# Turning q and k with transposing DMAs on 16-bit halves instead of TensorE transposes

## The reference

```python
for l in range(DEPTH):
    h = rms_norm(x, norm_mix[l])
    z = h @ w_in[l]
    qa, ka, va, qb, kb, vb, uc, gz = jnp.split(z, SPLIT_POINTS, axis=-1)
    qa = apply_axial_rope(rms_norm(qa.reshape(b, s, A_Q_HEADS, HEAD_DIM), qn_a[l]), ang_row, ang_col)
    ka = apply_axial_rope(rms_norm(ka.reshape(b, s, A_KV_HEADS, HEAD_DIM), kn_a[l]), ang_row, ang_col)
    ya = dense_gqa_blocked(qa, ka, va) @ w_branch_a[l]
    qb = apply_rope(rms_norm(qb.reshape(b, s, B_HEADS, HEAD_DIM), qn_b[l]), ang_seq)
    kb = apply_rope(rms_norm(kb.reshape(b, s, B_HEADS, HEAD_DIM), kn_b[l]), ang_seq)
    # B: three groups of four heads, each a dilated window; combined by their softmax denominators
    ...
    gates = jax.nn.sigmoid(gz + b_gate[l]).reshape(b, s, N_BRANCHES, D_MODEL)
    merged = gates[:, :, 0] * ya + gates[:, :, 1] * yb + gates[:, :, 2] * yc
    x = x + merged @ w_out[l]
    h2 = rms_norm(x, norm_ffn[l])
    x = x + (jax.nn.silu(h2 @ w_ffn_gate[l]) * (h2 @ w_ffn_up[l])) @ w_ffn_down[l]
```

## Time and profile before

| | us |
|---|---|
| runs: median (lowest to highest) | 822.84 (822.7 to 823.5) |
| profiled execution, device time | 823.74 |
| its span, first to last instruction | 821.9 |
| TensorE busy | 816.8 |
| VectorE busy | 574.0 |
| ScalarE busy | 436.4 |
| GpSimd busy | 239.3 |

### The profile page before, as it was taken

The page is one execution under the profiler, slowest core; times in us unless marked ns, Lnnn a source line. Parts: engine busy times, 40 slices in busy tenths (PEclk is TensorE's granted clock), DMA queues, the critical chain, the costliest instruction groups (busy, mean ns, idle before and its releaser), DMA issues.

```text
span 821.9 us, 9923 instructions
## 1 busy us (share of the span) xinstructions
PE 816.8 (99%) x3884; PEld 667.4 (81%) x3884; DVE 574.0 (70%) x688; ACT 436.4 (53%) x505; POOL 239.3 (29%) x206
## 2 busy tenths in 40 slices
PE   9999999999999999999999999999999999999998
PEld 7887778888888888888888877878888888888886
DVE  5999776667776767664379996677586767666552
ACT  6767755573364454543456686555734544444430
POOL 1342324230023444430023241524200444444200
PEclk9999999999999999999999999999999999999999
DMA  9756687685557676676455467677644566776661
GB/s 343 273 188 179 182 204 203 189 221 171 188 174 230 221 214 200 225 243 215 161 198 203 156 186 198 192 201 204 199 181 177 198 213 224 230 223 206 204 209 43
DMA packets 80142, 165.76 MB, mean 202 GB/s; under 512 B 59840, under 2 KB 60000, under 8 KB 62688
## 3 DMA queue, kind: packets, MB, share of 16 engines
q1 hardware_dynamic: 78176, 158.88, 61.3%
q0 software_dynamic: 1632, 6.18, 2.2%
q10 hardware_dynamic: 288, 0.08, 0.0%
HBM read 149.91 MB, written 1.05 MB: 184 GB/s over the span
## 4 chain that ended last, share of the span: by engine, by line
PE 98%; DMA 1%; DVE 0%; ACT 0%; SPq 0%; issue 0%
PE bank L1036 30%; PE bank L1038 30%; PE bank L1047 30%; PE bank L1069 2%; PE bank L1163 2%; PE bank L1140 1%; PE bank L1131 1%; PE bank L1104 1%; DMA x_sb<-in_x_dram 1%; PE bank L1110 0%; DVE w_lo L755 0%; PE bank L1173 0%; ACT w_hi L591 0%; ACT aT_hi L601 0%; DVE scratch L779 0%; DVE x_sb L931 0%
## 5 line engine op out<-in xcount | busy, mean ns | idle before, releaser
L755 DVE TENSOR_TENSOR w_lo<-w_raw,w_hi 128x2048 fp32r<-128x2048 f32 x134 | 317.8, 2374 | 97.5 <-ACT w_hi L591 97.1
L591 ACT ACTIVATE w_hi<-w_raw 128x2048 fp32r<-128x2048 f32 x134 | 256.3, 1915 | 155.5 <-DMA w_raw<-in_stream_dram 155.3
L1036 PE MATMUL bank<-w_hi,aT_hi 128*128 128x512 f32 x832 | 330.3, 397 | 0.0
L1038 PE MATMUL bank<-w_hi,aT_lo 128*128 128x512 f32 x832 | 324.7, 390 | 0.0
L1047 PE MATMUL bank<-w_lo,aT_hi 128*128 128x512 f32 x832 | 223.6, 391 | 0.1
L1036 PEld LDWEIGHTS bank<-w_hi,aT_hi 128*128 128x128 f32 x832 | 156.4, 188 | 37.3 <-issue 5.7
L1047 PEld LDWEIGHTS bank<-w_lo,aT_hi 128*128 128x128 f32 x832 | 155.6, 188 | 33.1 <-DVE w_lo L755 0.7
L1038 PEld LDWEIGHTS bank<-w_hi,aT_lo 128*128 128x128 f32 x832 | 156.6, 188 | 31.4
L539 POOL COPY hT_raw<-turned 128x512 uint16<-128x512 uint16 x44 | 35.6, 853 | 135.1 <-DMA turned<-halves 135.1
L530 POOL COPY halves<-hid 128x512 uint16<-128x512 uint16 x44 | 71.8, 1660 | 4.5 <-DVE hid L1008 4.5
L1036 PE MATMUL bank<-w_hi,hT_hi 128*128 128x512 f32 x176 | 68.7, 390 | 0.0
(11 more groups left out here) (98 smaller groups left out, 745.4 us busy)
## 6 DMA issues: line engine op xcount, KB each, us to landing
w_raw<-in_stream_dram SPq DMA_DIRECT2D x135, 1024.0 KB, 4.8
bias_sb<-in_b_gate_dram POOLq DMA_DIRECT2D x12, 256.0 KB, 3.5
par<-in_params_dram POOLq DMA_DIRECT2D x3, 384.0 KB, 3.5
w_raw<-in_stream_dram SPq DMA_DIRECT2D x4, 256.0 KB, 5.3
pool_mat<-in_pooling_dram POOLq DMA_DIRECT2D x1, 1024.0 KB, 7.5
out_dram<-x_sb SPq DMA_DIRECT2D x4, 256.0 KB, 4.2
x_sb<-in_x_dram SPq DMA_DIRECT2D x2, 256.0 KB, 4.1
x_sb<-in_x_dram SPq DMA_DIRECT2D x1, 512.0 KB, 6.3
```

The lines of the kernel that those rows point to most:

```text
L591: nc.scalar.activation(w_hi[:, j % RING, :, :].rearrange("p k n -> p (k n)"), w_raw[:, j % RING, :, :].rearrange("p k n -> p (k n)"), ACT. ...
L755: nc.vector.tensor_tensor(w[0], w[1], w[2].bitcast(F32), ALU.subtract).then_inc(unit_lo, 1)
L1036: nc.tensor.matmul(o, src[0][:, k, tok], w_hi[:, slot, wk + i, :], start=first and i == 0, stop=False)
L1038: nc.tensor.matmul(o, src[1][:, k, tok], w_hi[:, slot, wk + i, :], start=False, stop=False)
```

## The change

The nine batches of transposes per layer and their copies out of PSUM are gone. Each of the six regions, for each token half, takes the road of the probabilities:

- ScalarE splits the rotated region into halves, in iteration t of the unit after next (region rotated in unit t - 2), into a new buffer `head_halves` (`split_heads`).
- SP issues a transposing DMA, behind the weight load of that iteration and ahead of the transposes of probabilities (`turn_heads`). It lands in the region's own place in `zqk`.
- The halves are joined into `qkT`: A's two regions by ScalarE in units 7 and 8, B's four by GpSimd in units 13 to 16 (`join_heads`, by `JOIN_UNITS`).
- TensorE waits for A's joins at the first scores (unit 9), and for B's at the scores of pair 4 (unit 17). ScalarE waits for GpSimd's joins at two places where it overwrites the rooms.

```diff
+JOIN_UNITS = (7, 8, 13, 14, 15, 16)
...
-QK_BATCH = [(0, 2), (2, 2), (4, 1), (5, 2), (7, 2), (9, 2), (11, 2), (13, 2), (15, 2)]
+HEAD_TILES = [(0, 4), (4, 1), (5, 2), (7, 4), (11, 4), (15, 2)]
...
+            def turn_heads(lay, r, m):
+                sp.wait_ge(heads_split, lay * TURNED + (MT * r + m + 1))
+                sp.dma_start_transpose(turned_room(r, m).rearrange("p (g t) -> p g t", t=P), split_room(r, m)
+                                       ).then_inc(heads_turned[r], 16)
...
+                for n in range(TURNED):
+                    if lay >= 0 and REGIONS[n // MT][-1][n % MT] == t - 2:
+                        turn_heads(lay, *divmod(n, MT))
                 if lay >= 0 and pair_at(t, 1) is not None:
                     turn_probs(lay, pair_at(t, 1))
...
+            def join_heads(lay, r, m):
+
+                pool.wait_ge(heads_turned[r], (lay + 1) * 16 * MT)
+                nc.gpsimd.tensor_copy(joined_heads(r, m), turned_heads(r, m)).then_inc(late_heads_joined, 1)
...
+                    for r in range(2, len(REGIONS)):
+                        if JOIN_UNITS[r] == t:
+                            for m in range(MT):
+                                join_heads(lay, r, m)
...
-                elif kind == "qk":
-                    first, k = QK_BATCH[i]
-                    free(nc.scalar.activation(qkT[:, first:first + k, :].rearrange("p k n -> p (k n)"),
-                                              B(name)[:, 0:k * SEQ], ACT.Copy), name)
...
+            def split_heads(lay, n):
+
+                r, m = divmod(n, MT)
+                first, k = HEAD_TILES[r]
+                act.wait_ge(rotated, lay * TURNED + (n + 1))
+                both = zqk[:, m, P * first:P * (first + k)].bitcast(U16).rearrange("p (f h) -> p h f", h=2)
+                nc.scalar.activation(split_room(r, m).rearrange("p (h f) -> p h f", h=2), both, ACT.Copy
+                                     ).then_inc(heads_split, 1)
...
                     for j in splits_at(t, ahead=3):
                         split(lay, j)
+                    for n in range(TURNED):
+                        if REGIONS[n // MT][-1][n % MT] == t - 2:
+                            split_heads(lay, n)
+                    for r in range(2):
+                        if JOIN_UNITS[r] == t:
+                            for m in range(MT):
+                                join_heads(lay, r, m)
...
                 if p == 0:
-                    wait_emptied(pe, lay, ("qk", 2))
+                    pe.wait_ge(heads_joined, lay * 4 + 4)
                 if p == 4:
-                    wait_emptied(pe, lay, ("qk", 7))
-                    wait_emptied(pe, lay, ("qk", 8))
+                    pe.wait_ge(late_heads_joined, lay * 8 + 8)
```

More of the change, by code:

```diff
@@ L252, in build @@
         pool_mat = sb("pool_mat", [P, MT, POOL_G, SEQ])
+        with ExitStack() as shared:
+            head_halves = sb("head_halves", [P, 20 * MT * 2 * P], U16, shared)
         mixT_hi = sb("mixT_hi", [P, POOL_G, SEQ], F32R)
@@ L326, in build @@
         hidden_ready = sem("hidden_ready")
+        heads_split = sem("heads_split")
+        heads_turned = [sem(f"heads_turned{r}") for r in range(len(REGIONS))]
+        heads_joined = sem("heads_joined")
+        late_heads_joined = sem("late_heads_joined")
         vchain = sem("vchain")
@@ L403, in probs_part, with split_room, turned_room, turned_heads @@
             return probs[:, i % 2, :]
+        def split_room(r, m):
+            first, k = HEAD_TILES[r]
+            at = 2 * P * (MT * ((first + 8) % 19) + m * k)
+            return head_halves[:, at:at + 2 * P * k]
+        def turned_room(r, m):
+            first, k = HEAD_TILES[r]
+            return zqk[:, m, P * first:P * (first + k)].bitcast(U16)
+        def turned_heads(r, m):
+            return turned_room(r, m).rearrange("p (h k t) -> p h k t", h=2, t=P)
+        def joined_heads(r, m):
+            first, k = HEAD_TILES[r]
+            return qkT[:, first:first + k, P * m:P * m + P].bitcast(U16).rearrange("p k (t h) -> p h k t", h=2)
         block = ctx.enter_context(nc.Block())
@@ L599, in turn @@
                     wait_emptied(act, lay, name)
+                    if name == ("mixed", 0):
+                        act.wait_ge(late_heads_joined, lay * 8 + 8)
                     src = scratch[:, NC * (n % 2):NC * (n % 2) + NC]
@@ L651, in split_probs, with join_heads @@
                                      ).then_inc(probs_split, 1)
+            def split_heads(lay, n):
+                r, m = divmod(n, MT)
+                first, k = HEAD_TILES[r]
+                act.wait_ge(rotated, lay * TURNED + (n + 1))
+                both = zqk[:, m, P * first:P * (first + k)].bitcast(U16).rearrange("p (f h) -> p h f", h=2)
+                nc.scalar.activation(split_room(r, m).rearrange("p (h f) -> p h f", h=2), both, ACT.Copy
+                                     ).then_inc(heads_split, 1)
+            def join_heads(lay, r, m):
+                act.wait_ge(heads_turned[r], (lay + 1) * 16 * MT)
+                nc.scalar.activation(joined_heads(r, m), turned_heads(r, m), ACT.Copy).then_inc(heads_joined, 1)
             def x_squares(lay, m, half):
@@ L1088, in transposes @@
                         last = turn(P * k, merged[:, m, P * (UK * half + k):P * (UK * half + k + 1)])
-                elif kind == "qk":
-                    first, k = QK_BATCH[i]
-                    region = (0, 0, 1, 2, 3, 3, 4, 4, 5)[i]
-                    pe.wait_ge(rotated, lay * TURNED + 2 * (region + 1))
-                    for j in range(k):
-                        for m in range(MT):
-                            last = turn(P * (2 * j + m), zqk[:, m, P * (first + j):P * (first + j + 1)])
                 elif kind == "pool":
```

8 lines of the change are left out of this document (4 added, 4 removed).

## The result

The changed kernel takes **833.82 us** (median of four runs, 832.0 to 836.64) against 823.17 us for the kernel before beside it (822.7 to 823.88): a ratio of 1.013 with the 95% interval [1.010, 1.017]. It is 1.3% slower. The forecast was 828.1 us with a range of 815 to 835, so sign, mechanism and place held, and the size was 5.7 us short: a rise of 5.3 us was forecast and 10.7 us were measured.

The account below looks back on a forecast made before the run. TensorE, busy 816.8 of 821.9 us, was taken as the bound, with VectorE close behind. From the median 822.84: - 8.0 work + 2 x 6.35 gates wait + 0.6 z6 copy = + 5.3, so 828.1 us, range 815.0 to 835.0.

Parts of the forecast that it names:

- TensorE's work: Transposes on TensorE: eight batches of four at 0.47 us and one half-size per layer go, 8.0 us less in the kernel.
- The alternation: Units 13 and 14: GpSimd's copies and VectorE's operations take turns, one instruction each, each waiting for the other's whole.
- Six short operations: VectorE, units 13 and 14: four L891 and two L862, 2.2 us with reciprocals, each meeting one 1.3 us GpSimd copy.
- the first rival: Whole kernel: copies fall beside operations that don't contend or VectorE goes ahead; gain whole, 814.8 to 815.4 us, chance 0.16.
- The size of the wait: Start of unit 16: TensorE waits 6.35 us per layer for the gates, which end at 111.8 us.
- w_hi for unit 17: ScalarE: stands behind the last head split and two splits of probabilities, takes 1.8 us, done at 107.4 us.
- the main case: Units 13 to 16: six short operations meet six large copies, the last normalisation takes 1.45 us; stall 6.35 us per layer.
- the bad end of 9.95 us: Unit 16: joins of pair 2 and b_k1 also meet the last normalisation, 3.6 us more, stall 9.95 us.
- ScalarE at the first scores: Unit 9: ScalarE done with A's joins at 59.4, TensorE ready at 60.2; wait 0, at worst 0.5 us per layer.
- The copy of z6: Start of unit 14: copy leaves its PSUM bank 0.1 to 0.7 us late, 0.6 us for both layers together.
- the third rival: Unit 17: TensorE waits for GpSimd's last join, 1 to 2 us per layer; chance 0.16 shared with 1 to 4 us stalls.
- Nothing is lost there: Weight loads on SP: 1.3 to 4 us late behind head transposes, but 9 us of cover before unit 16, no loss.

Follow-up runs that it names:

- e8: Changed kernel with only B's heads turned by DMA, all B's joins on ScalarE where it idles, A's three batches transposed by TensorE as before: 819.22 us, ratio 0.995.
- e6: Changed kernel with GpSimd's joins of b_k0 moved from unit 15 to 16, behind the probabilities of pair 2: 835.93 us, ratio 1.014.
- e1: Changed kernel with B's joins moved from GpSimd to ScalarE, in the same units 13 to 16: 831.27 us, ratio 1.010.

## Why the prediction was right, and where it was short

**TensorE's work.** 8.0 us less was forecast, 7.1 us measured. TensorE was ready for unit 16 at 105.73, forecast 105.45, but that is closer than the term was: 0.76 us of it came from the faster start of this execution. The batch of four was priced 0.47 us from a single pair of rows. A's batches cost that in the first layer (1.2 us for two and the small one), B's six cost 0.40 each in e8, where TensorE hardly waits (93.50 - 91.08 = 2.42 us less from unit 1 to unit 16).

**The alternation.** Six short operations and six copies in a row, one each, were forecast. In the second layer it was so but for one: five of the short operations and w_lo met the six copies. Two L957 in 2.6 and two L928 in 2.9 us were forecast at 2 x 1.3 to 1.5. With a copy waiting, VectorE never had two of the operations that it holds up in a row, so the first rival, whole gain, fell.

**The size of the wait.** Forecast 6.35 us per layer with bounds of 4.0 and 9.95; measured 3.90 and 5.71. The step that was too large was to let all six meet in both layers, when in the first the transposes landed late. The step behind it, w_hi for unit 17, stood behind the last head split as forecast, but was taken too late: it was put at 105.6, 0.15 us behind the moment at which TensorE is ready for unit 16, and began 6.4 us ahead of that moment in the first layer (99.29 against 105.73) and 3.4 us ahead in the second (509.69 against 518.80 - 5.71 = 513.09). The term is 9.6 where the sum had 12.7: 3.1 too much.

That it came so close is in part luck, as neither layer went the way of the main case. There the six short operations of units 13 and 14 meet copies and the last normalisation doesn't. In the first layer only the last normalisation met them (2.61 + 2.54 us instead of 0.62 + 0.62, 3.9 us more), in the second both did (the last for 2.55 + 1.41 us, 2.7 us more). Both ways stood among the bounds, the second as the bad end of 9.95 us. That it cost 5.71 instead goes with the early w_hi and the one operation that slipped through; the rows don't split it further.

**The clock.** The term that is missing altogether. The kernel before ran at full clock from 10 us on, and no row of it showed what a wait does to it. Each wait of this kind brought 3.4 to 6.8 us at 1.2 GHz and so 4.0 us in all. It made up for more than the smaller wait. The result stayed inside the range of 815 to 835 only because the range's upper end had been set by longer waits, which didn't come: that too is luck. A sum of stalls alone is too small here by some 40% of the stalls.

**ScalarE at the first scores.** Forecast 0 with 0.5 per layer as the bad end; measured 0.53 and 0.71. One mis-sized term is the join, which writes 16-bit halves with a stride. Two took 2.43 us from their start to that of the next instruction, priced 1.9 by the split of the earlier trace rows, and the small pair 0.68, priced 0.6: 0.6 us together. That alone doesn't make the wait, as the forecast had 0.8 us to spare (59.4 against 60.2). In the first layer ScalarE was done at 59.87, and TensorE, faster from the start of the execution, was ready at 59.48. The second layer's wait wasn't taken apart.

**The copy of z6.** Forecast 0.6 us; no wait at the start of unit 14. Its first half left its bank at 91.5, forecast 92.5: the row maxima of pair 2 were at 88.28, not 89.2 (0.8 us of that is the faster start of this execution), and TensorE, with 0.8 us from the same source, came at the 92.2 that was forecast.

**Values.** Three waits of TensorE for joined probabilities, 1.5 us together, weren't in the sum; the third rival looked at GpSimd's lateness only at the scores of unit 17. In e6, with b_k0's two copies there as well, that one does appear (0.9 us). In the changed kernel it doesn't.

**The weights.** "Nothing is lost there" was half right. No matmul waited for weights. But SP's timeline in the first layer shows the load behind the transposes, and those of ScalarE and VectorE who waits for it:

```profile
84.90 1.23 SPq L474 DMA_TRANSPOSE zqk<-head_halves  x1
86.24 7.19 SPq L469 DMA_TRANSPOSE gates<-scratch  x2
93.48 4.62 SPq L480 DMA_DIRECT2D w_raw<-in_stream_dram  x2
```

```profile
99.29 1.92 ACT L636 ACTIVATE w_hi<-w_raw 128x2048 fp32r<-128x2048 f32 x1 [1.53 <-DMA w_raw<-in_stream_dram]
101.12 0.45 ACT L673 ACTIVATE probs<-bank,neg_max 128x256 f32<-128x256 f32 x1
```

```profile
101.24 2.32 DVE L821 TENSOR_TENSOR w_lo<-w_raw,w_hi 128x2048 fp32r<-128x2048 f32 x1 [1.12 <-ACT w_hi L636]
```

Two probability transposes hold SP for 7.19 us where it was 5.39. That a head transpose goes ahead of them doesn't explain it by itself: in the second layer one does too, and the two take 5.24 us. The cause stays open. ScalarE then waits 1.53 us for the weights of unit 17, and VectorE 1.12 us for ScalarE. The cover was counted to the matmuls and not to the next engine that reads the load. By these rows up to 1.1 us of the first layer's 3.90 comes from there; no run had SP free of it, so that share is argued and not shown.

**The sum again**, in the forecast's form and, as it was made against a profiled execution, from its 829.0: - 3.1 for the gates, + 4.0 clock, + 1.2 and 1.5 for scores and values, - 0.6 for z6, + 0.9 for the work that didn't go, - 0.8 for the faster start: 832.1. The profiled execution took 832.65. The median of the runs lies 1.2 above that; the two slower ones, 834.98 and 836.64 us, had a lower mean clock (0.992 and 0.987 against 0.994), but weren't profiled.

## What to carry to other kernels

Before work is moved to GpSimd, look for VectorE's SBUF operations in the same stretch, and count one whole GpSimd instruction for each of them that can meet one; big copies beside many short operations cost most here, and the same copies cost nothing as long as the engine behind still had cover. When the bound is TensorE running without a gap, price a longer stall as its length plus the slower matmuls after it (here 1.7 to 2.3 us behind stalls of 3.3 to 5.7 us, nothing behind those up to 1.6 us). And count a late load's cover to the first engine that reads it, in that engine's own order, not to the matmul at the end.

## What the runs showed of the hardware that was not expected

- After a wait of 1.94, 3.33 or 3.90 us TensorE's granted clock was at the 1.2 GHz level for 3.4 us, and for 6.8 us with waits of 5.71 and 6.29 us. The wait's length alone doesn't set it: in e1 a wait of 4.37 us went with 6.8 us at the lower level and one of 4.44 us with 3.4 us. It didn't fall at once: behind the 3.90 us wait the first matmuls still started every 0.23 us, and 0.43 came 1.2 us later. Behind waits of 0.5 to 1.56 us it stayed full.
- In every stretch read here GpSimd's copies and VectorE's operations from SBUF to SBUF alternated, one each, for as long as both had work: beside 1.4 us copies a 0.35 us operation took 1.2 to 1.5 us and a 2.28 us one 3.38 us, six times in a row, and also when nothing read the copies.
- ScalarE joined 1,024 halves in 1.22 us from start to start where it split as many in 0.95.
- In one execution of e6 the two layers, with the same instructions, waited 0.4 and 6.3 us for the gates. What the timelines show to differ is when pair 1's transposes landed: 2.2 us behind the start of VectorE's short operations in the one, 0.07 us in the other. That this alone decides is argued from the timelines and not tested.
